# Feed-forward up and gate projections computed feature-major in a two-block transformer kernel

## The reference, cut to what matters

```
first block:   h2 = rms_norm(x, g_mlp)
               x  = x + square(relu(h2 @ w_ff1)) @ w_ff2          # 1024 -> 4096 -> 1024
second block:  x  = x + 0.5 * swiglu(rms_norm(x, ffn1_norm), ...)  # 1024 -> 2816 -> 1024
               ...
               x  = x + 0.5 * swiglu(rms_norm(x, ffn2_norm), ...)
swiglu(x, w_gate, w_up, w_down) = (silu(x @ w_gate) * (x @ w_up)) @ w_down
rms_norm(x, g) = x * rsqrt(mean(x*x) + eps) * g
```

## Time and profile before

| | |
|---|---|
| median of 3 runs | 1019.78 us (1019.32 to 1019.88) |
| the profiled execution's own time | 1019.78 us |
| its span in the profile | 1018.0 us |
| TensorE busy | 992.1 us, 97% of the span, 4730 matmuls |
| VectorE busy | 578.5 us, 57% |
| ScalarE busy | 489.1 us, 48% |
| GpSimd busy | 72.3 us, 7% |
| DMA | 179 MB, mean 176 GB/s |

### The profile page before, as it was taken

The page is one execution under the profiler, slowest core; times in us unless marked ns, Lnnn a source line. Parts: engine busy times, 40 slices in busy tenths (PEclk is TensorE's granted clock), DMA queues, the critical chain, the costliest instruction groups (busy, mean ns, idle before and its releaser), DMA issues.

```text
span 1018.0 us, 12693 instructions
## 1 busy us (share of the span) xinstructions
PE 992.1 (97%) x4730; PEld 821.4 (81%) x4730; DVE 578.5 (57%) x700; ACT 489.1 (48%) x613; POOL 72.3 (7%) x95
## 2 busy tenths in 40 slices
PE   6999999999999999999999999999999999999997
PEld 4888788888888888888778888888877888888885
DVE  4655555487675555555775455447555675555443
ACT  5545455744355344444563434335557454444431
POOL 3100000040020000000320000001111000000000
PEclk9999999999999999999999999999999999999999
DMA  9755545444465555454555555545552165556531
GB/s 322 249 193 167 163 134 187 144 154 186 165 238 207 192 186 185 171 200 166 203 174 202 177 195 183 188 149 176 175 204 65 44 208 184 196 177 205 168 122 42
DMA packets 99744, 179.27 MB, mean 176 GB/s; under 512 B 5856, under 2 KB 53872, under 8 KB 99696
## 3 DMA queue, kind: packets, MB, share of 16 engines
q1 hardware_dynamic: 97424, 171.99, 48.7%
q0 software_dynamic: 1984, 6.30, 2.0%
q10 hardware_dynamic: 288, 0.33, 0.1%
HBM read 177.55 MB, written 1.05 MB: 175 GB/s over the span
## 4 chain that ended last, share of the span: by engine, by line
PE 93%; DVE 3%; ACT 1%; issue 1%; POOL 1%; DMA 1%; DVEq 0%; POOLq 0%; ACTq 0%
PE bank L467 84%; PE bank L481 5%; PE bank L517 1%; PE bank L516 1%; DVE w_lo L1309 1%; DMA masks<-const_masks 1%; PE bank L528 0%; PE bank L530 0%; PE bank L529 0%; POOL rs L1813 0%; POOL ms L1812 0%; DVE x L1561 0%; PE bank L794 0%; PE bank L793 0%; DVE sg L1560 0%
## 5 line engine op out<-in xcount | busy, mean ns | idle before, releaser
L1309 DVE TENSOR_TENSOR w_lo<-raw,w_hi 128x2048 fp32r<-128x2048 f32 (+2 forms) x163 | 370.9, 2280 | 221.0 <-ACT w_hi L920 220.9
L920 ACT ACTIVATE w_hi<-raw 128x2048 fp32r<-128x2048 f32 (+2 forms) x163 | 308.1, 1891 | 159.9 <-PE bank L467 157.2
L467 PE MATMUL bank<-w_hi,hA_hi 128*128 128x512 f32 (+1 forms) x880 | 343.0, 396 | 5.1 <-DVE w_lo L1399 3.0
L467 PE MATMUL bank<-w_hi,hA_lo 128*128 128x512 f32 (+1 forms) x880 | 337.1, 389 | 0.0
L467 PE MATMUL bank<-w_lo,hA_hi 128*128 128x512 f32 (+1 forms) x880 | 336.7, 389 | 0.0
L467 PEld LDWEIGHTS bank<-w_hi,hA_hi 128*128 128x128 f32 x880 | 165.4, 188 | 38.7 <-issue 4.7
L467 PEld LDWEIGHTS bank<-w_hi,hA_lo 128*128 128x128 f32 x880 | 165.6, 188 | 34.7
L467 PEld LDWEIGHTS bank<-w_lo,hA_hi 128*128 128x128 f32 x880 | 165.9, 188 | 32.4
L467 PE MATMUL bank<-w_hi,fT_hi 128*128 128x512 f32 x304 | 93.8, 390 | 0.0
L467 PE MATMUL bank<-w_lo,fT_hi 128*128 128x512 f32 x304 | 93.6, 389 | 0.0
L467 PE MATMUL bank<-w_hi,fT_lo 128*128 128x512 f32 x304 | 93.6, 389 | 0.0
(11 more groups left out here) (236 smaller groups left out, 759.3 us busy)
## 6 DMA issues: line engine op xcount, KB each, us to landing
raw<-in_w_in SPq DMA_DIRECT2D x76, 512.0 KB, 4.5
raw<-in_w_ff SPq DMA_DIRECT2D x64, 512.0 KB, 3.9
raw<-in_ffn_w_gate SPq DMA_DIRECT2D x44, 512.0 KB, 3.6
raw<-in_ffn_w_up SPq DMA_DIRECT2D x44, 512.0 KB, 4.5
raw<-in_ffn_w_down SPq DMA_DIRECT2D x44, 512.0 KB, 4.0
raw<-in_w_out SPq DMA_DIRECT2D x16, 512.0 KB, 3.8
raw<-in_w_branch_diff SPq DMA_DIRECT2D x8, 512.0 KB, 3.7
raw<-in_w_branch_ret SPq DMA_DIRECT2D x8, 512.0 KB, 3.7
```

Source lines behind the costliest of these rows:

```text
L467: mm = pe.matmul(o, a, w, start=first and t == 0 and m < len(outs), stop=last and t == n - 1 and m >= len(todo) - len(outs))
L920: act.activation(w_hi[u % HI_SLOTS][:, 0:w], raw[u % RAW_SLOTS][:, 0:w], ACT.Copy).then_inc(hi_ready, 1)
L1309: vec.tensor_tensor(w_lo[u % RAW_SLOTS][:, 0:w], raw[u % RAW_SLOTS][:, 0:w], w_hi[u % HI_SLOTS][:, 0:w].bitcast(f32), ALU.subtract).then_i ...
```

## The change

The up and gate products of the three feed-forward layers are computed feature-major: a 128x128 piece of the weight is stationary and the activations of all 256 tokens stream past it. `hA_hi` and `hA_lo` now lie in one tensor `hA2`, so that one matmul with `w_hi` stationary streams 512 columns, 256 of high and 256 of low activations, into the two halves of one bank; a second matmul with `w_lo` stationary streams the 256 high columns into the first half. DVE adds the two halves (`tensor_reduce`). Four such tiles of 128 features (banks 4 to 7) make a step. Since the result has its features on the partitions, it is split into `fT` without a transpose: all 152 transposes go.

The norm factor of a token now lies along the columns. In "ff" it moves behind the down product (`x_add` with `rs2`). In "f1" and "f2" the gate needs it before silu: POOL writes two diagonal matrices, TensorE multiplies them by ones into bank 0 (so that every partition holds all 256 factors), DVE copies that to `rsb` and multiplies each gate tile by it; the up half's factor moves behind the down product together with the 0.5 (`rsh`, made by POOL). The first product of a layer does the same tiles for 128 tokens at a time: 256 columns with `w_hi`, 128 columns with `w_lo`. The transposes of the normalised rows of "mlp", "ffn1" and "ffn2" go to banks 0 to 3. In "f1", `lo` of the second unit of the next stage moves behind the first `x_add`.

```diff
-    hA = [sb(f"hA_{s}", [P, KT, SEQ], f32r) for s in ("hi", "lo")]
+    hA2 = sb("hA", [P, 2, KT, SEQ], f32r)
+    hA = [hA2[:, 0], hA2[:, 1]]
...
-    up = lambda tb: bank[4 + tb]
+    tall = lambda f: bank[4 + f]
+    halves = lambda f: tall(f)[:, :].rearrange("p (s t) -> p s t", t=SEQ)
...
+    def work(name):
+        if name[0] in ("mlp", "ffn1", "ffn2"):
+            return acc(name[1], name[2])
+        return bank[0] if name[0] == "p" else bank[6 + WB[name] % 2]
... TensorE
+        def tall_product(f, u, t, kt, cols, first, last):
+            at = t * HALF + f * P
+            hi, lo = w_hi[u % HI_SLOTS][:, at:at + P], w_lo[u % RAW_SLOTS][:, at:at + P]
+            both = halves(f)[:, :, cols], hi, hA2[:, :, kt, cols]
+            one = halves(f)[:, 0, cols], lo, hA2[:, 0, kt, cols]
+            for m, operands in enumerate((one, both) if last else (both, one)):
+                mm = pe.matmul(*operands, start=first and m == 0, stop=last and m == 1, skip_group_check=True)
+            return mm
+
+        def first_tiles(name, norm, order, beside=None):
+            u, s = U0[name], STEP0[name]
+            if s:
+                pe.wait_ge(up_out, TILES * s)
+            for tb in range(TB):
+                cols = slice(tb * P, (tb + 1) * P)
+                for j in range(2):
+                    turned((norm, tb, j))
+                    if tb and j and beside:
+                        beside()
+                    pe.wait_ge(lo_ready, u + j + 1)
+                    for n, f in enumerate(order):
+                        for t in range(4):
+                            mm = tall_product(f, u + j, t, 4 * j + t, cols, (tb, j, t) == (0, 0, 0),
+                                              (tb, j, t) == (1, 1, 3))
+                        if tb and j and n < TILES - 1:
+                            mm.then_inc(up_done, 1)
+                    if tb:
+                        mm.then_inc(unit_used, 1)
+                    if (tb, j) == (0, 0):
+                        src_turn(norm, 1)
+
+        def tiles(name, u, i, order, du=0, ds=0):
+            s = STEP0[name] + i
+            for j in range(2):
+                pe.wait_ge(lo_ready, u + j + 1 + du)
+                for n, f in enumerate(order):
+                    if j == 0:
+                        pe.wait_ge(up_out, TILES * (s - 1) + n + 1 + TILES * ds)
+                    for t in range(4):
+                        mm = tall_product(f, u + j, t, 4 * j + t, slice(0, SEQ), (j, t) == (0, 0), (j, t) == (1, 3))
+                    if j and n < TILES - 1:
+                        mm.then_inc(up_done, 1)
+                mm.then_inc(unit_used, 1)
...
+            def rstd_rows():
+                pe.wait_ge(ones_ready, 1)
+                pe.wait_ge(diag_ready, TB * (GATED[name] + 1))
+                for tb in range(TB):
+                    mm = pe.matmul(bank[0][:, tb * P:(tb + 1) * P], ones[:, :], diag[:, tb, :], start=True, stop=True)
+                mm.then_inc(rsb_done, 1)
+            first_tiles(name, norm, PAIRED, rstd_rows)
... ScalarE
-            act.activation(act_r[:, tb, :], up(tb)[:, :], ACT.Relu, scale=rs2[:, tb:tb + 1]).then_inc(act_ready, 1)
+        def f_split(name, i, k, slot, dr=0):
+            act.wait_ge(act_ready, ROW0[name] + TILES // (2 if name in GATED else 1) * i + k + 1 + dr)
+            act.activation(fT[0][:, slot, :], act_f[:, k, :], ACT.Copy).then_inc(f_hi, 1)
...
+                act.wait_ge(gate_in, PAIR0[name] + 2 * i + k + 1 + 8 * r)
+                act.activation(act_r[:, k, :], act_s[:, k, :], ACT.Silu).then_inc(gate_out, 1)
... VectorE
+        def tile_sum(name, i, n, f, dst, last_unit, ds=0, du=0):
+            s = STEP0[name] + i
+            if n < TILES - 1:
+                vec.wait_ge(up_done, (TILES - 1) * s + n + 1 + (TILES - 1) * ds)
+            else:
+                vec.wait_ge(unit_used, last_unit + 1 + du)
+            vec.tensor_reduce(dst, tall(f)[:, :].rearrange("p (s t) -> p t s", t=SEQ), axis=mybir.AxisListType.X,
+                              op=ALU.add).then_inc(up_out, 1)
+            vec.wait_ge(up_out, TILES * s + n + 1 + TILES * ds)
+        def square(i, f, r=0):
+            tile_sum("ff", i, f, f, act_s[:, f, :], U0["ff"] + 1 + (4 * i - 2 if i else 0), 3 * r, 12 * r)
+            vec.scalar_tensor_tensor(out=act_f[:, f, :], in0=act_s[:, f, :], scalar=0.0, in1=act_s[:, f, :],
+                                     op0=ALU.max, op1=ALU.mult).then_inc(act_ready, 1)
...
+            def multiply(i, k, r=0):
+                last_unit = u + 1 + (3 * i - 1 if i else 0)
+                tile_sum(name, i, 2 * k, k, act_s[:, k, :], last_unit, 4 * r, 12 * r)
+                vec.tensor_tensor(act_s[:, k, :], act_s[:, k, :], rsb[:, :], ALU.mult).then_inc(gate_in, 1)
+                tile_sum(name, i, 2 * k + 1, 2 + k, act_s[:, 2 + k, :], last_unit, 4 * r, 12 * r)
+                vec.wait_ge(gate_out, PAIR0[name] + 2 * i + k + 1 + 8 * r)
+                vec.tensor_tensor(act_f[:, k, :], act_r[:, k, :], act_s[:, 2 + k, :], ALU.mult).then_inc(act_ready, 1)
+            vec.wait_ge(rsb_done, GATED[name] + 1)
+            vec.tensor_copy(rsb[:, :], bank[0][:, 0:SEQ]).then_inc(rsb_ready, 1)
... GpSimd, behind the norm factors of "ffn1" and of "ffn2"
+        def rstd_rows(name, k):
+            for tb in range(TB):
+                n = SQ[name, tb]
+                pool.wait_ge(rstd_ready, n + 1)
+                pool.tensor_scalar(diag[:, tb, :], ident, rs[:, n:n + 1], None, ALU.mult).then_inc(diag_ready, 1)
+            for tb in range(TB):
+                n, m = SQ[name, tb], 2 * k + tb
+                h = pool.tensor_scalar(rsh[:, m:m + 1], rs[:, n:n + 1], 0.5, None, ALU.mult)
+            h.then_inc(rsh_ready, 1)
```

216 lines of the change are left out of this document (96 added, 120 removed).

## The result

The changed kernel takes 1028.44 us (median of six runs, 1026.03 to 1032.31) where the kernel before, in runs on the same chip, takes 1019.83 (1019.32 to 1020.01): a ratio of 1.009 with a 95% interval of 1.0066 to 1.0113. It is 8.6 us slower. The forecast was 1021 us, called no clear change on the slow side, with "slower" as the likeliest sign at 51%; 1028.4 lies inside the range of 1012 to 1032, and 7.4 us above the point.

The account below looks back on a forecast made before the run. TensorE bounds the kernel: number of matmuls times the distance between starts. Terms -4.9 - 4.9 - 0.9 - 1.0 - 0.4 + 3.9 + 4.7 + 4.5 = +1.0 us on 1019.78 gave 1020.8, called 1021; range 1012 to 1032.

Parts of the forecast that it names:

- the forecast case: Whole kernel: the terms hold as summed, 1017 to 1024 us; chance 48%.
- all four rivals: Narrow products pay full width (17%), VectorE becomes the bound (13%), floor fails for fp32r (17%), transposes' time returns as waits (5%).
- narrow pieces of up to 133 ns in the steady steps: Steady steps' 256-column matmuls cost 133 ns, not 120: +11.5 us over 864 pieces, 1032; shares 13% with VectorE as bound.
- the forecast's own signs of being wrong: Forecast is wrong if a steady step lengthens, or the three first products together don't cost 11 to 14 us.
- Steady steps: Up products split in two widths, transposes gone: -0.70 us in each of seven "ff" steps, -0.27 in 18 others.
- The narrow floor: First products: a 128-column matmul costs 111.5 ns, set by the stationary load; +3.9 at "mlp", +4.7 at "f1", +4.5 at "ffn2".
- Both rivals on the price of narrow fp32r matmuls: First products' 128-column matmuls cost up to 227 ns (1043 us, 17%), or 67 ns (1012 us; 17% with milder forms).
- The head of "f1": First product of "f1": +4.7 us, with a 1.45 us wait of TensorE for the diagonals; first quarter inside an existing wait.
- VectorE and ScalarE: Steps: VectorE busy 12.0 of 16.5 us in "f1", 15.4 of 22.0 in "ff"; sums 0.69 us, costed at nothing.
- The rival in which VectorE becomes the bound: Slow sums or late subtractions make "f1" steps run at VectorE's pace: 13 us, 1034; 13% with the 133 ns form.
- Last steps: Ends of layers: -0.9 us in "ff", -0.5 each in "f1" and "f2" including 0.25 of waiting, -0.4 for `src`.
- The rival in which their 0.44 us come back as waits: Steps: transposes' time returns as TensorE waits for sums, +0.21 us a step, total about +12, 1032; chance 5%.

Follow-up runs that it names:

- grouped kernel: Changed kernel with the steady steps' matmuls grouped by sixteen, so that one narrow stretch stands in a step; 1026.84 us, ratio 1.0067.
- gain early: Changed kernel with the gain of "ffn1" loaded during the end of "ff", so GpSimd's product of two gains starts earlier; 1027.5 us, ratio 1.007.
- all edits together: Changed kernel with grouping by sixteen, gain loaded early, norm factors' product behind the first product, and whole second halves in first products; 1018.83 us, ratio 0.9987.
- the kernel before with an idle piece: Kernel before, with one wait added so TensorE starts the first product of "f1" later; 1022.86 us, ratio 1.0028.
- sums first: Kernel with all edits together, and VectorE taking all four sums before its wait for the norm factors; 1016.15 us, ratio 0.9963.

## Why the prediction was right in its sign and short in its size

**What bounds the kernel: right.** TensorE's starts set the time of both kernels; every microsecond above is a distance of starts, an idle piece or the clock of TensorE.

**How far it held.** The total lies in the range, but none of the named cases happened: the forecast case had 1017 to 1024 for itself, and all four rivals fall. The room up to 1032 was made for two of those rivals, and for narrow pieces of up to 133 ns in the steady steps. That 1028.4 lies inside is in part luck. One of the forecast's own signs of being wrong also came: the three first products together cost 3.8 + 7.4 + 4.3 = 15.5 us and not 11 to 14. 0.65 us of the total is the first load at the start, which landed after 5.9 us in one profile and 5.3 in the other, ahead of anything that the change touches.

**Steady steps: the term that was mis-sized.** I forecast -9.8 us for 25 steps (-0.70 and -0.27 each) and the traces give 7 x (-0.52) + 18 x (-0.09) = -5.3. The single prices were right: 226.7 and 120.0 ns are what the grouped kernel shows for long rows. The error was to add them as if a matmul's price didn't depend on its neighbour. The earlier trace rows had the hint, a slow start behind each group of transposes, which I booked as going away with them (0.04 us). In fact the trace of before has, behind its four transposes, six wide starts of 229 to 235 ns, not one late one. The change removed one such disturbance a step and put 32 in its place. It costs 5.3 ns a pair, 0.17 us a step; over 25 steps that is 4.2 of the 7.5 us that were missing.

**The narrow floor: right.** A pair of 256 and 128 columns in the first products takes 230.6 ns: the 96 matmuls in 14.96 us at 524.62 are the last quarter and a step's product of 11.27, which leaves 3.69 us for 16 pairs (231.5 ns forecast, 340 and 187 for the rivals). The first product of "ff" came to +3.8 us (3.9 forecast), that of "f2" with its product with ones to +4.3 (4.5). Both rivals on the price of narrow fp32r matmuls, 17% each, fall. The Trainium skill's rule on the load of a stationary piece ("TensorE: Matmul & The Clock Gate", "LDWEIGHTS", 107 ns for 128 columns) agrees with the 110.6 ns that a pair leaves for its 128-column matmul. The 2.5 ns between back-to-back matmuls, which the Trainium skill gives on the same page under "Back-to-back issue gap", don't agree, here as in the forecast: 512 and 256 columns in long rows carry 13.3 ns each.

**The head of "f1": the mechanism right, the size short by 2.7 us.** The wait for the diagonals was 1.77 us (1.45 forecast): GpSimd took 0.6 us for each diagonal, where about 0.4 was put. Moving the product with ones away removed the wait. What was not in the sum came from a seam that I had taken as fixed: GpSimd's gain product landed on VectorE's first operation and made TensorE 1.6 us late against its matmuls ahead (508.49 - 503.01 against 507.01 - 503.11 before). The forecast said that the first quarter lies inside a wait that is there anyway; that assumed its start. And the idle piece of 2.5 us brought the clock to its lower level, which made the first quarter 5.44 - 3.70 = 1.7 us longer; 0.9 of it stood out behind the wait for the second block. With the 0.3 us of the wait for GpSimd that is 1.6 + 0.9 + 0.3 = 2.8, against the 2.7. The meeting was shown by taking it away (gain early), and the fall went with it; a fall was also brought about by an idle piece alone, in the kernel before. Neither is a fixed price of the change: in the profiles a meeting of more than 0.3 us stands only where the gain's load takes over 5 us.

**VectorE and ScalarE: right.** 11.56 us of a step where 12.0 were forecast, sums of 685 ns, and no wait of TensorE for them in the steps. The rival in which VectorE becomes the bound (13%) falls for this order of work. It is less far off than I put it: grouped by sixteen, the last steps wait 0.8 us each, and behind the first product a sum that is one place late costs over a microsecond.

**Last steps: right.** The 0.25 us of waiting that I put behind the last tile didn't come in the changed kernel; no wait for `fT` stands in it. The 0.4 us wait for the first block's `src` is gone; one of 0.2 us came at the transposes of the next.

**Transposes go: right.** The rival in which their 0.44 us come back as waits (5%) falls.

**The spread.** The changed kernel's runs lie at 1026.0 to 1026.5, 1028.4 and 1031.9 to 1032.3, with mean granted clocks of 0.998, 0.9965 and 0.9935. The profiled run, with one fall of 3.4 us, is of the middle group. The profiled run holds a meeting of 1.65 us and 0.9 us of clock, and without both it would stand at 1025.9. So the lowest group is most likely made of runs with neither, and not of runs that lack only the fall; the highest would be runs with a longer fall or more of them. That is what the times and the mean clocks suggest; only one run of this kernel was profiled.

The 1013.8 us forecast for all edits together were 5.0 us short of 1018.83. Of these the stalls behind the first products are 2.7 and the grouping 0.9 (4.5 was put and 3.6 came). The remaining 1.4 is close to the 1.5 of the early gain. That forecast took it off 1026.0, the changed kernel's fastest runs, and these most likely had no meeting to remove: the kernel with the early gain alone has 1026.17 as its own fastest run.

Left open: why wide matmuls are late behind narrow ones, which no experiment here reached below the level of starts; and why the gain's load takes 4 us in some runs and 5 in others.

## What to carry to other kernels

Price a matmul among its neighbours: where wide and narrow ones alternate, or transposes stand between, group them, and check the starts by their place in the row. Replacing few transposes by splitting a product in two widths was nearly a draw here; it paid only with the narrow ones in long rows and with the next stage's sums taken in time. At a seam, list what each engine has in flight when the late operand arrives: here a GpSimd product that came 1.4 us later (2.6 us with the clock, in the runs where it does), and a product with a late operand queued ahead of a quarter that had its operands (1.8 us), cost 4 us between them, as much as the grouping gives. And where the runs of one kernel fall in groups, compare group with group, and take a saving only off a run that had the loss.

## What the runs showed of the hardware

- fp32r matmuls with a new stationary piece each, at the 2.4 GHz level: 512 columns 226.7 ns, 256 columns 120.0 ns in long rows; 256 and 128 columns alternating 230.6 ns a pair.
- Behind a narrow stretch (256 columns, or transposes) about five wide ones are longer, by 27 ns in all behind 32 narrow ones; with alternation each wide one stays at 235 ns and each narrow one at 117.
- GpSimd's tensor product of 1024 columns (2.38 us) stretched a VectorE operation of 0.69 us to 2.31 us when that started 0.6 us into it, and to 0.83 us when it started 0.3 us before its end.
- At the head of "f1" the granted clock went to 0.50 (1.2 GHz) in all five profiles with 2.3 to 2.6 us without a matmul (for 3.4 us in three, 6.8 in two), and with 3.8 us (for 3.4) and 4.2 us (for 6.8). With 1.8 us it fell in one profile of five (for 6.8), with 0.9 to 1.0 us in none.
- In the attention part it fell for 3.4 us in two profiles of twelve (the kernel before with an idle piece near 814, "sums first" near 806.5), where no idle piece is longer than 1.0 us, and the idle pieces are the same in profiles without a fall.
- A load of 512 KB, issued at the same place, landed after 3.8 to 4.1 us in three profiles and after 5.1 to 5.4 in five.
- A moving operand in two pieces 8 KB apart streams like a contiguous one (11.27 us for the 64 matmuls either way).
